# Moving operands whose rows stand 1040 bytes apart instead of 1024

## What is computed

```python
def first_block(x, ...):
    proj = rmsnorm(x, attn_norm_w) @ w_in                 # 1024 -> 3072
    y = group_rmsnorm(concat(stick_breaking, chunked_attention, conv), out_norm_w)
    x = x + y @ w_out
    h = rmsnorm(x, ffn_norm_w)
    return x + (silu(h @ w_gate) * (h @ w_up)) @ w_down   # 1024 -> 2816 -> 1024

def second_block(x, ...):
    proj = rms_norm(x, mix_norm_g) @ w_in                 # 1024 -> 5888
    merged = gates[0] * (y_a @ w_branch_a) + gates[1] * (y_b @ w_branch_b)
    x = x + merged @ w_out
    up = rms_norm(x, ffn_norm_g) @ w_up                   # 1024 -> 2 * 2816
    x = x + (gelu(conv(up_a)) * up_v) @ w_down
    return rms_norm(x, final_norm_g)
```

## Time and profile before

| | us |
|---|---|
| median of 3 runs (lowest, highest) | 733.24 (732.87, 733.75) |
| the profiled execution, its own time | 733.58 |
| its span, first to last instruction | 731.6 |
| TensorE busy in the span | 711.8 |
| VectorE busy | 457.8 |
| ScalarE busy | 377.4 |
| GpSimd busy | 48.9 |

### The profile page before, as it was taken

The page is one execution under the profiler, slowest core; times in us unless marked ns, Lnnn a source line. Parts: engine busy times, 40 slices in busy tenths (PEclk is TensorE's granted clock), DMA queues, the critical chain, the costliest instruction groups (busy, mean ns, idle before and its releaser), DMA issues.

```text
span 731.6 us, 13005 instructions
## 1 busy us (share of the span) xinstructions
PE 711.8 (97%) x5570; PEld 676.8 (93%) x5570; DVE 457.8 (63%) x677; ACT 377.4 (52%) x572; POOL 48.9 (7%) x42
## 2 busy tenths in 40 slices
PE   6979999999999999999999999999999999999996
PEld 4768899999999999998988888899999999999996
DVE  6764476787766664454574445558689878886431
ACT  7735673654544454445445545444466665564421
POOL 2030112200000000003000000000030000000000
PEclk9989999999999999999999999999999999999999
DMA  8843314264555465535454433254725554555401
GB/s 299 330 153 112 116 66 166 116 231 173 183 205 190 173 234 200 200 120 205 173 180 166 173 116 116 86 183 144 280 114 181 188 210 175 173 190 213 173 2 57
DMA packets 19961, 123.70 MB, mean 169 GB/s; under 512 B 2240, under 2 KB 3776, under 8 KB 5696
## 3 DMA queue, kind: packets, MB, share of 16 engines
q1 hardware_dynamic: 18000, 120.59, 45.7%
q10 hardware_dynamic: 1904, 2.28, 1.0%
HBM read 121.82 MB, written 1.05 MB: 168 GB/s over the span
## 4 chain that ended last, share of the span: by engine, by line
PE 88%; DMA 4%; issue 3%; DVE 2%; POOL 1%; ACT 1%; SPq 0%; POOLq 0%; DVEq 0%; ACTq 0%
PE pm L301 42%; PE psc L301 33%; PE ptr L301 9%; DMA raw<-in_w_dram 2%; PE po L301 2%; PE ptr L304 2%; DMA bias<-in_rel_dram 2%; DVE xl L316 1%; POOL acc L313 1%; POOL tiny L313 0%; ACT p L310 0%; DVE p L1348 0%; ACT wh L310 0%; ACT sq L310 0%; DVE x L313 0%
## 5 line engine op out<-in xcount | busy, mean ns | idle before, releaser
L313 DVE TENSOR_TENSOR wl<-raw,wh 128x1024 fp32r<-128x1024 f32 (+1 forms) x230 | 276.9, 1218 | 47.8 <-ACT wh L310 40.3
L310 ACT ACTIVATE wh<-raw 128x1024 fp32r<-128x1024 f32 (+1 forms) x230 | 232.9, 1035 | 47.5 <-PE psc L301 21.1
L301 PE MATMUL pm<-xh,wh 128*128 128x256 f32 x560 | 159.3, 284 | 0.1
L301 PE MATMUL pm<-xh,wl 128*128 128x256 f32 x560 | 156.6, 280 | 0.0
L301 PE MATMUL pm<-xl,wh 128*128 128x256 f32 x560 | 156.2, 279 | 0.0
L301 PEld LDWEIGHTS pm<-xh,wh 128*128 128x128 f32 x560 | 105.4, 188 | 2.2 <-issue 1.8
L301 PEld LDWEIGHTS pm<-xl,wh 128*128 128x128 f32 x560 | 105.4, 188 | 0.0
L301 PEld LDWEIGHTS pm<-xh,wl 128*128 128x128 f32 x560 | 105.2, 188 | 0.0
L301 PE MATMUL psc<-xh,wh 128*128 128x256 f32 x304 | 85.2, 280 | 0.1
L301 PE MATMUL psc<-xh,wl 128*128 128x256 f32 x304 | 85.1, 280 | 0.0
L301 PE MATMUL psc<-xl,wh 128*128 128x256 f32 x304 | 84.7, 279 | 0.0
(11 more groups left out here) (261 smaller groups left out, 1317.5 us busy)
## 6 DMA issues: line engine op xcount, KB each, us to landing
raw<-in_w_dram SPq DMA_DIRECT2D x111, 1024.0 KB, 4.8
raw<-in_w_dram SPq DMA_DIRECT2D x3, 512.0 KB, 7.5
bias<-in_rel_dram ACTq DMA_DIRECT2D x1, 1024.0 KB, 12.2
out_dram<-raw SPq DMA_DIRECT2D x4, 256.0 KB, 2.5
x<-in_xt_dram SPq DMA_DIRECT2D x3, 256.0 KB, 6.6
raw<-in_w_dram SPq DMA_DIRECT2D x2, 256.0 KB, 4.2
bbc<-in_bsp_dram ACTq DMA_DIRECT2D x1, 384.0 KB, 3.2
cbs<-in_cb_dram ACTq DMA_DIRECT2D x1, 352.0 KB, 8.5
```

The lines of the kernel that those rows point to most:

```text
L301: return lambda e: e.matmul(dst, lhs, rhs, start=start, stop=stop, skip_group_check=True)
L310: return lambda e: e.activation(dst, src, kind, **kw)
L313: return lambda e: e.tensor_tensor(dst, a, b, op)
```

## The change

The rows of `xh`, `xl`, `hh` and `hl` get 260 elements instead of 256, and only the first 256 are used. The views handed to the rest of the program have the same shape, so nothing else in the code differs.

```diff
+WIDE = SEQ + 4
...
-        xh = keep("xh", [P, KT, SEQ], f32r)
-        xl = keep("xl", [P, KT, SEQ], f32r)
+        xh = keep("xh", [P, KT, WIDE], f32r)[:, :, 0:SEQ]
+        xl = keep("xl", [P, KT, WIDE], f32r)[:, :, 0:SEQ]
...
-        (hh, hl), e2 = region(base, ("hh", [P, FT, SEQ], f32r), ("hl", [P, FT, SEQ], f32r))
+        (hh, hl), e2 = region(base, ("hh", [P, FT, WIDE], f32r), ("hl", [P, FT, WIDE], f32r))
+        hh, hl = hh[:, :, 0:SEQ], hl[:, :, 0:SEQ]
```

## The result

The changed kernel takes 736.1 us at the median of 7 runs (735.84 to 740.04). The kernel before, run beside it, takes 732.91 (732.55 to 733.83). The ratio is 1.0052 with a 95% interval of 1.0035 to 1.0070: half a per cent slower, clear of the noise. It was forecast at 736.2 with slower the likeliest.

What follows compares the result with a forecast made beforehand. TensorE, busy 97% of the span, was taken as the bound. Terms of +2.65, +0.51 and -0.21 us summed to +2.95, giving 736.2 us against the median of 733.24, with a range of 730.0 to 742.0.

Steps and rivals of the forecast that it cites:

- TensorE's pace is the whole of it, and the writers are free: Whole kernel: time is matmul count times pace plus unchanged waits; ScalarE and VectorE writes to the moved tiles add nothing.
- The place of a moving row sets its pace, 32 being good and the others 118.33: Matmuls moving `xh`, `xl`, `hh`, `hl`: start within 128 bytes decides; 32 gives 116.67 or 117.78 ns, others 118.33.
- The sum: All stages with moved tiles together: +2.95 us, giving 736.2 us against the median of 733.24.
- The first feed and its like: First feed and other stages moving `xh` or `xl`: seven rows in eight leave 32, +1.66 ns a matmul, +2.65 us.
- The second feed: Second feed, moving `xh` and `xl`: seven rows in eight leave 32, +0.55 ns a matmul, +0.51 us.
- The down projections: Down projections, moving `hh` and `hl`: some rows come to 32, 128 matmuls gain 1.66 ns each, -0.21 us.
- No change: Rival, all matmuls: pace doesn't depend on a tile's start, the three paces are rhythms; 733.2 us, 28%.
- Split pieces: Rival, moved rows at 16 or 48: one extra 32-byte piece, 3.65 ns each, +7.2 us, 740.4 us, 10%.
- Collisions with the weights: Rival, 984 moved rows at the weights' place within 64 bytes: 10 ns more each, +9.8 us, 743.0 us, 6%.
- Faster by breaking the pattern: Rival, second feed and down projections: spread places break a regular pattern, all reach 116.67 ns; 730.3 us, 20%.

Runs made afterwards that it cites:

- x_at_96: Against the kernel before, `xh` and `xl` keep 1024-byte rows and move by 64 bytes, tiles behind them by 128; 744.38 us, ratio 1.0153.
- scan_b: Against the kernel before, five groups of activation tiles shifted to odd multiples of 16 within 256 bytes, pitch 1024; one execution 734.22 us beside 732.94.

## Why the prediction was right, and where it was not

The number was right (736.2 against 736.1), and the sign. That it came within 0.1 us is luck: the cost was put at 2.95 us and came to 3.2 between the medians, and the kernel before, run beside it, was 0.3 us under the 733.24 from which the forecast started. By its own steps:

- *TensorE's pace is the whole of it, and the writers are free.* Right. The writers stayed at 418 ns, no wait changed, and the paces account for 3.6 us.
- *The place of a moving row sets its pace, 32 being good and the others 118.33.* Right that the place decides, wrong in what the place is, and this is the step that failed although the number came out. The period is 256 bytes, not 128, and the weights' place counts as much as the row's. The other places aren't alike either: they run from 113.3 to 120.0 at multiples of 16. The forecast took three samples of a curve (distances 32, 224 and, for moving weights, 224 again) and called the second and third a rule.
- *The sum.* The first feed and its like were put at +2.65 us and measured 2.05 + 1.10 = 3.15. The second feed was put at +0.51 and measured +0.88. Both are larger because the pace came to 118.61 and not to about 118.1. The down projections were put at -0.21 and measured -0.12. The gain on 512-column matmuls, -0.35, was not foreseen. Against the 3.6 us traced, the errors cancel in part, and 118.33 happens to lie near the mean of the curve (118.0). A change that moved all rows to one new place would have been forecast badly: x_at_96 was put at 1.005 and came to 1.0153.
- *What was given to the rivals.* 'No change' is out, since uniform shifts alone gave 0.980 to 1.015. Split pieces are out by scan_b. Collisions with the weights: at distance 0, 120.0 is 3.3 ns over 116.67 and not 10, and distances 64, 128 and 192, which have the same place within 64, aren't bad. 'Faster by breaking the pattern' had it the wrong way round: a pace under 116.67 exists, but by standing regularly at one distance.

The two rules that the prediction weighed can be judged now. Moving `xh` by 64 bytes, four whole pieces of 16, cost 1.5% with its neighbours' shift (x_at_96), and in the table 16 bytes, from 96 to 112, change the pace by 6.7 ns. The Trainium skill's rule of 16-byte lines (Advanced Engine Details and Errata, SBUF Cachelines) would have all of these alike. The measurement decides against it as a full account for this kind of matmul. Moving the weights alone took the down projection from 118.33 to 120.0 ns. The Trainium skill's two independent read ports of TensorE (SBUF — State Buffer, Who interferes with whom) would have that at 0, and the measurement decides against it: whatever the ports are, the pace here depends on both addresses.

## What to carry to other kernels

When TensorE is busy throughout, divide the length of unbroken matmul runs by their count for each stage. Stages of one instruction form that differ by 1% may be a sign that addresses matter, though the two feeds before differ as much at identical addresses. Then test uniform shifts of one operand by multiples of 16 bytes, several tiles to one run, before spreading rows over places: the two spreads over eight places tried here came within 0.3 and 0.7 ns of the average of the curve, and a single good distance gives its best value. Check what a shift moves behind it, because padding that looks neutral within 128 bytes was not.

## What the runs showed of the hardware

With TensorE's granted clock at 1.00, float32r matmuls of 256 columns with one weight load each run at 113.3 to 130.0 ns, depending mainly on the moving operand's start less the stationary operand's, within 256 bytes. At one distance stages differ by up to 1.3 ns among uniform placements at multiples of 32, by 2 at 16 and by 9 at 104. The best distance of those tried is 112 bytes (113.3), the worst multiples of 16 are 0 and 96 (120.0), and 4 to 8 bytes off the best cost 6.7 to 16.7 ns. Since every weight block stands at one place, the runs can't tell whether a matmul's own weights count or those loaded beside it. With 512 columns of weights moving, the mean distance of starts was 230 to 234 ns over the uniform placements, so there the place counts less. Why 112 is good was not found.
